# Output stage of a hybrid transformer step: three weight slots instead of four, expert weights requested there one by one

## The chip, the cores and the metric

The kernel runs on one core of one Trainium2 chip. The metric is the device time of one execution in microseconds (us); the figure to compare is the median of several runs. A profile of one execution, with a record of every instruction and DMA packet, stands beside it.

## The reference

One layer of a diffusion backbone in float32, for two streams ("samples") of 128 tokens and 2048 channels:

```
mod = silu(c) @ w_ada + b_ada            # 6 x 2048 values per stream: shift1, scale1, gate1, shift2, scale2, gate2
h   = rmsnorm(x) * (1 + scale1) + shift1
u, q, k, v, g_a, g_b = split(h @ w_in + b_in)
merged = sigmoid(g_a) * (fourier(u) @ w_fourier) + sigmoid(g_b) * (attention(q, k, v) @ w_na_o)
x1  = x + gate1 * (merged @ w_out)                       # the output stage
t   = rmsnorm(x1) * (1 + scale2) + shift2
group = argmax(t @ w_router_group); two best of the 4 experts of that group by t @ w_router_expert
y   = sum over the two experts: weight * ((silu(t @ w_gate[e]) * (t @ w_up[e])) @ w_down[e])
out = rmsnorm(x1 + gate2 * y)
```

There are 16 experts; their three matrices are 4 MB each, 192 MB in all, and every run reads all of them. The rest of the weights is about 220 MB.

## The kernel before, in words

**Dense stages.** Every weight matrix before the experts is read in loads of 1 MB (4 tiles of 128 rows by 512 columns). A load `l` is split by two units, `2*l` and `2*l+1`, of half a load each: ScalarE (ACT) writes the rounded part `w_hi` (`high(u)`, L1370), VectorE (DVE) the remainder `w_lo` (`low(u)`, L1724), and TensorE (PE) multiplies both (`unit(l, half)`, L827 to L829: 12 matmuls of 512 columns). `high(u)` waits until unit `u-4` was used, so ACT and DVE work at most four units ahead. `L_OUT` = 80 is the first load of the output stage `merged @ w_out`, `L_ALL` = 96 the end. Four loads make a chunk of 512 output columns; the stage's chunks are 24 to 27, in banks 0 and 1 or 2 and 3 by turns. When a chunk is complete DVE reads it (`read_chunk`: times gate L1850, plus x L1856), which it counts on `chunk_read`.

**The ring.** Dense loads go to `raw`, four slots of 8 KB a partition (`RAW` = 4). Between them, up to load 77, stands one load of `w_ada` for each dense load: `ada_super(a)` multiplies it with the conditioning vector (L808, 4 matmuls). 64 such loads (a = 32 to 95) share the ring, the last four (a = 92 to 95, `LATE_ADA` = 4) behind the last dense load. Load `n` of the ring has slot `n % 4`, and waits until the slot's previous load was split or multiplied (`slot_released`). SyncE's queue (SP) issues the loads up to 83. From load 84 on ACT issues load `l + 4` in its step `l`, ahead of `high(2*l+4)`.

**Experts.** Expert matrices come in 192 loads of 1 MB in the order in which PE uses them. `MRAW` = 11 slots take them by turns: `mraw` slots 0 to 3 lie over `w_hi` and `w_lo`, 4 to 7 over the four `raw` slots, and `mraw_g`, `mraw_x`, `mraw_y` stand apart. Loads 12 to 15 have single-use places: 12 and 15 in `mraw_a`, 13 and 14 in `mraw_f`, which lies over the upper 16 KB of region F, where `x1T` (the transposed x1) lies too. All are issued by SP in one fixed order (`first_gate_up_load`, L574 on); a wait in it holds up all that stands behind it. From load 11 on each waits until PE has used the load that had its slot (`slot_free`, L546).

**Routing.** x1 is transposed chunk by chunk (`x1_transposes`, L1017; ACT copies it into `x1T`, L1522), and `router(n, s)` (L1027) multiplies chunk `n` of sample `s` with the router's weights, in banks 2 and 3. So `router(0, ...)` first waits until chunk 26 was read out of these banks. After the last load PE does routers 2 and 3, two late `ada_super`, the ranks of the chosen experts (L1109 to L1111), two more `ada_super`, then gathers tokens (L1135) and begins with the experts (gate and up L1196, down L1235, scatter L1277).

Of the kernel before, what the change touches and what calls it, by code (L numbers as in the profile page):

```python
# [13 lines left out]
P = 128  # L14
TOK = 128
# [105 lines left out]
def backbone_step(nc, x_prompt, x_sample, cache_k, cache_v, c, c_ctx, norm1_g, norm2_g, w_ada, b_ada,  # L121
# [24 lines left out]
    with ExitStack() as ctx:  # L146
# [43 lines left out]
        x1T = place("x1T", [P, KD, NS, TOK], F + 16 * KB)  # L190
# [157 lines left out]
        LATE_ADA = 4  # L348
# [10 lines left out]

        def landed_count(n):  # L360

            return 16 * (n // RAW) + 16
# [110 lines left out]
        def slot_released(queue, n):  # L473

            if n >= RAW:
                queue.wait_ge(raw_done[n % RAW], 8 * (n // RAW))

        def ada_super_load(queue, a):

            n = ADA_AT[a]  # L480
            super_chunk, k = GATE1 + (a - A_SUPER) // KD, (a - A_SUPER) % KD
            slot_released(queue, n)
            queue.dma_start(raw[:, n % RAW].rearrange("p (a k) n -> p a (k n)", a=1),
                            ada_v[:, k:k + 1, super_chunk * D:(super_chunk + 1) * D]).then_inc(raw_landed[n % RAW], 16)

        def dense_load(queue, l):

            n = DENSE_AT[l]
            chunk, quad, _ = chunk_of(l)
            if l < L_MERGE:  # L490
                view, col = in_v, PROJ_COLS[chunk]
            elif l < L_OUT:
                i, kind = (chunk - 8) // 4, (chunk - 8) % 4
                view = (in_v, in_v, na_v, fo_v)[kind]
                col = i * COL + (FW + 3 * NA, FW + 3 * NA + D, 0, 0)[kind]
            else:
                view, col = out_v, (chunk - 24) * COL
            slot_released(queue, n)
            queue.dma_start(raw[:, n % RAW], view[:, LOAD_K * quad:LOAD_K * quad + LOAD_K, col:col + COL]
                            ).then_inc(raw_landed[n % RAW], 16)  # L500
# [5 lines left out]
        def _(sp):  # L506
# [67 lines left out]
            with sp.Fori(0, rounds_end) as r:  # L574
# [3 lines left out]

                first_gate_up_load(9)
                first_gate_up_load(10)  # L580
                sp.wait_ge(chunk_read, reads(21))
                first_gate_up_load(8)
                sp.wait_ge(unit_used, 2 * L_ALL - 4)
# [5 lines left out]
                sp.wait_ge(raw_done[0], 8 * (RING_LOADS // RAW))  # L589
# [192 lines left out]
        def _(pe):  # L782
# [13 lines left out]
            def ada_super(a):  # L796

                n = ADA_AT[a]
                super_chunk, k = GATE1 + (a - A_SUPER) // KD, (a - A_SUPER) % KD
                if k == 0:  # L800

                    if super_chunk == GATE1:
                        pe.wait_ge(mod_ready, BLOCKS - 1)
                    else:
                        pe.wait_ge(ada_evac, super_chunk - GATE1)
                pe.wait_ge(raw_landed[n % RAW], landed_count(n))
                for g in range(4):
                    last = nc.tensor.matmul(bank[7][32 * g:32 * g + 32], cpad[:, k], raw[:, n % RAW, g],  # L808
                                            start=k == 0, stop=k == KD - 1)
                last.then_inc(raw_done[n % RAW], 8)  # L810

            def unit(l, half):
# [8 lines left out]
                pe.wait_ge(raw_done[n % RAW], 8 * (n // RAW) + 4 * half + 4)  # L821
# [10 lines left out]
            def last_load(l):  # L832
# [3 lines left out]
                pe.wait_ge(raw_done[n % RAW], 8 * (n // RAW) + 8)  # L836
# [201 lines left out]
            for l in range(L_LOOP, L_ALL - 1):  # L1038
# [37 lines left out]
                if l == L_ALL - 3:  # L1076
                    router(0, 1)
# [26 lines left out]
            for a in (92, 93):  # L1104
                ada_super(a)
# [254 lines left out]
        def _(act):  # L1360
            step = Tally(act, act_step)
            def high(u):

                n = DENSE_AT[u // 2]
                if u % 2 == 0:
                    act.wait_ge(raw_landed[n % RAW], landed_count(n))
                if u >= AHEAD:
                    act.wait_ge(unit_used, u - AHEAD + 1)
                r = raw[:, n % RAW, (u % 2) * UNIT_K:(u % 2) * UNIT_K + UNIT_K]
# [74 lines left out]
            def super_done(super_chunk):  # L1444

                n = ADA_AT[A_SUPER + KD * (super_chunk - GATE1) + KD - 1]
                act.wait_ge(raw_done[n % RAW], 8 * (n // RAW) + 8)
# [72 lines left out]
            def x1_transposed(n, s):  # L1520
                act.wait_ge(x1T_done, 2 * n + s + 1)
                nc.scalar.activation(x1T[:, 4 * n:4 * n + 4, s], bank[x1T_bank(n, s)][:].rearrange("p (k t) -> p k t", k=4), ACT.Copy  # L1522
# [192 lines left out]
        def _(dve):  # L1715
# [3 lines left out]
            def low(u):  # L1719
# [3 lines left out]
                r = raw[:, n % RAW, (u % 2) * UNIT_K:(u % 2) * UNIT_K + UNIT_K]  # L1723
                v.tensor_tensor(w_lo[:, u % AHEAD], r, w_hi[:, u % AHEAD].bitcast(F32), ALU.subtract  # L1724
                                ).then_inc(raw_done[n % RAW], 4)
# [393 lines left out]
            dve.wait_ge(raw_done[n % RAW], 8 * (n // RAW) + 8)  # L2119
# [185 lines left out]
```

## Time and profile before

| | us |
|---|---|
| three runs, median | 1196.16 |
| three runs, lowest and highest | 1195.09, 1196.16 |
| the profiled execution, its own time | 1196.65 |
| span of the profile, first to last instruction | 1194.8 |
| PE busy (5577 matmul records) | 1116.9 (93%) |
| DVE busy, ACT busy | 535.9, 366.3 |
| 64 `in_w_in` loads, issue to landing (median) | 8.3 |
| 46 `in_w_exp_gate` loads, issue to landing (median) | 20.8 |

Positions such as "at 680 us" count from the span's start. Busy time of PE is overlapped time of pipelined matmuls: 0.39 us is the duration of a 512-column matmul, but in a dense row of them one starts every 0.23 us (the 12 of a half load take 2.73 us). A float32 matmul stands in the trace as two records, so the 8 matmuls of two `ada_super` appear as x16. Idle time of an engine that nobody waits for costs nothing. "GB/s" is what all 16 DMA engines of the core moved together.

### The profile page before, as it was taken

The page shows a single profiled execution, that of the slowest core. Times are in us where ns is not written, and L with a number is a line of the kernel's source. Part 1 is how long each engine was busy: PE and PEld are TensorE (multiplying, and loading weights), DVE is VectorE, ACT ScalarE, POOL GpSimd, SP SyncE. Part 2 cuts the span into 40 slices and gives each one's busy share as a digit, 9 for nine tenths or more (in the row PEclk, how much of TensorE's full clock was granted, in tenths as well). Part 3 has the DMA queues.
Part 4 walks back from the last instruction along what each step waited for, and adds up shares of the span by engine and source line. Part 5 has one row for each costly group of instructions (what it writes and reads, how often), then busy time and mean ns, then how long its engine had stood idle before and what let it go on. Part 6 is the DMA issues. An engine that isn't in the chain of part 4 may idle for free.

```text
span 1194.8 us, 14481 instructions
## 1 busy us (share of the span) xinstructions
PE 1116.9 (93%) x5577; PEld 682.5 (57%) x5577; DVE 535.9 (45%) x781; ACT 366.3 (31%) x526; POOL 54.8 (5%) x100
## 2 busy tenths in 40 slices
PE   5899999999999999999999999999999888988795
PEld 2566766777777677667788875434344234423231
DVE  0464575555455444454466755242416041504056
ACT  3342342444433333333345533320112001201023
POOL 0210200110000220000010100000000000000000
PEclk9999999999999999999999999999999999999997
DMA  9999978887877898888898799999999999999994
GB/s 357 385 386 381 364 286 320 312 302 281 286 289 283 306 351 323 326 299 319 329 362 260 219 381 423 390 415 423 423 423 423 423 422 424 422 423 423 423 406 174
DMA packets 114964, 423.22 MB, mean 354 GB/s; under 512 B 9088, under 2 KB 9264, under 8 KB 82640
## 3 DMA queue, kind: packets, MB, share of 16 engines
q1 hardware_dynamic: 101968, 389.57, 83.4%
q0 software_dynamic: 5424, 15.35, 4.8%
q10 hardware_dynamic: 7504, 17.37, 4.0%
q8 instruction: 45, 0.74, 0.2%
q14 instruction: 23, 0.19, 0.0%
HBM read 418.27 MB, written 3.98 MB: 353 GB/s over the span
## 4 chain that ended last, share of the span: by engine, by line
PE 69%; DMA 27%; SPq 1%; DVE 1%; issue 1%; ACT 1%; DVEq 0%
PE bank L827 14%; PE bank L828 13%; PE bank L829 13%; PE bank L1196 10%; DMA mraw<-in_w_exp_up 10%; DMA mraw<-in_w_exp_down 5%; PE bank L808 5%; DMA raw<-in_w_in 4%; DMA mraw<-in_w_exp_gate 4%; PE bank L1235 3%; DMA raw<-in_w_ada 2%; PE bank L1135 2%; DMA mraw_y<-in_w_exp_gate 2%; PE bank L792 1%; PE bank L1277 1%; PE bank L1258 1%
## 5 line engine op out<-in xcount | busy, mean ns | idle before, releaser
L1724 DVE TENSOR_TENSOR w_lo<-raw,w_hi 128x1024 fp32r<-128x1024 f32 x192 | 231.8, 1223 | 246.7 <-ACT w_hi L1370 245.6
L1370 ACT ACTIVATE w_hi<-raw 128x1024 fp32r<-128x1024 f32 x192 | 200.3, 1057 | 313.3 <-DMA raw<-in_w_in 160.4
L827 PE MATMUL bank<-w_hi,h_hi 128*128 128x512 f32 x512 | 206.2, 403 | 6.6 <-DVE w_lo L1724 4.3
L828 PE MATMUL bank<-w_lo,h_hi 128*128 128x512 f32 x512 | 200.1, 391 | 0.0
L829 PE MATMUL bank<-w_hi,h_lo 128*128 128x512 f32 x512 | 199.8, 390 | 0.0
L1196 PE MATMUL bank<-mraw,xg 128*64 128x512 f32 x720 | 184.9, 597 | 12.5 <-DMA mraw<-in_w_exp_gate 4.8
L827 PEld LDWEIGHTS bank<-w_hi,h_hi 128*128 128x128 f32 x512 | 96.2, 188 | 47.1 <-issue 24.8
L1196 PEld LDWEIGHTS bank<-mraw,xg 128*64 128x64 f32 x720 | 57.7, 136 | 108.4 <-issue 105.6
L829 PEld LDWEIGHTS bank<-w_hi,h_lo 128*128 128x128 f32 x512 | 96.1, 188 | 21.0
L828 PEld LDWEIGHTS bank<-w_lo,h_hi 128*128 128x128 f32 x512 | 96.3, 188 | 18.1
L2190 DVE SCALAR_TENSOR_TENSOR d_lo<-bank,slot_w,d_hi 128x512 fp32r<-128x512 f32 x32 | 23.9, 747 | 161.6 <-ACT d_hi L1669 161.0
L1235 PE MATMUL bank<-mraw,hidT 128*64 128x512 f32 x336 | 84.3, 607 | 12.2 <-DMA mraw<-in_w_exp_down 12.2
L1669 ACT ACTIVATE d_hi<-bank,slot_w 128x512 fp32r<-128x512 f32 x32 | 22.0, 688 | 226.8 <-PE bank L1235 142.3
L2202 DVE TENSOR_TENSOR bank<-bank,ga2b 128x512 f32<-128x512 f32 x64 | 41.5, 694 | 77.1 <-PE bank L1277 77.0
L808 PE MATMUL bank<-raw,cpad 128*32 128x512 f32 x512 | 63.3, 610 | 2.8 <-DMA raw<-in_w_ada 2.8
L1235 PEld LDWEIGHTS bank<-mraw,hidT 128*64 128x64 f32 x336 | 26.9, 139 | 57.2 <-issue 52.7
L792 PE MATMUL bank<-araw,cpad 128*32 128x512 f32 x256 | 34.2, 643 | 14.8 <-DMA araw<-in_w_ada 14.8
L827 PE MATMUL bank<-w_hi,m_hi 128*128 128x512 f32 x120 | 47.7, 398 | 0.0
L829 PE MATMUL bank<-w_hi,m_lo 128*128 128x512 f32 x120 | 46.9, 390 | 0.0
L828 PE MATMUL bank<-w_lo,m_hi 128*128 128x512 f32 x120 | 46.7, 390 | 0.0
L2129 DVE TENSOR_TENSOR xg<-bank,rbi 128x512 f32<-128x512 f32 x32 | 21.9, 684 | 52.8 <-PE bank L1135 52.8
L1196 PE MATMUL bank<-mraw_g,xg 128*64 128x512 f32 x96 | 43.7, 598 | 1.6 <-DMA mraw_x<-in_w_exp_up 1.2
(293 smaller groups left out, 1332.2 us busy)
## 6 DMA issues: line engine op xcount, KB each, us to landing
raw<-in_w_in SPq DMA_DIRECT2D x64, 1024.0 KB, 8.3
raw<-in_w_ada SPq DMA_DIRECT2D x60, 1024.0 KB, 8.2
mraw<-in_w_exp_gate SPq DMA_DIRECT2D x46, 1024.0 KB, 20.8
mraw<-in_w_exp_up SPq DMA_DIRECT2D x44, 1024.0 KB, 20.9
mraw<-in_w_exp_down SPq DMA_DIRECT2D x42, 1024.0 KB, 20.6
araw<-in_w_ada SPq DMA_DIRECT2D x64, 512.0 KB, 10.9
raw<-in_w_out ACTq DMA_DIRECT2D x12, 1024.0 KB, 9.3
raw<-in_w_na_o SPq DMA_DIRECT2D x8, 1024.0 KB, 7.2
```

The source lines that it names most:

```text
L792: last = nc.tensor.matmul(bank[7 - b % 2][32 * g:32 * g + 32], cpad[:, 2 * j + g % 2], araw[:, n % ARAW, g], start=j == 0, stop=j == 7)
L808: last = nc.tensor.matmul(bank[7][32 * g:32 * g + 32], cpad[:, k], raw[:, n % RAW, g], start=k == 0, stop=k == KD - 1)
L827: nc.tensor.matmul(o, hi[:, k, s], wh, start=k == first, stop=False)
L828: nc.tensor.matmul(o, hi[:, k, s], wl, start=False, stop=False)
L829: last = nc.tensor.matmul(o, lo[:, k, s], wh, start=False, stop=k == final)
L1135: last = nc.tensor.matmul(out[:, kk * EPG * CAP:(kk + 1) * EPG * CAP], (t_hi, t_lo)[part][:, s, k * P:(k + 1) * P], pick[:, s, g * EPG:(g ...
L1196: last = nc.tensor.matmul(out[x * CAP:(x + 1) * CAP], xg[:, q * LOAD_K + kk, e * CAP:(e + 1) * CAP], slab(2 * unit + x)[:, kk * COL:(kk + ...
L1235: last = nc.tensor.matmul(bank[first_bank + n][x * CAP:(x + 1) * CAP], hidT[:, i % 2, k, x * CAP:(x + 1) * CAP], slab(2 * unit + x)[:, n * ...
L1370: nc.scalar.activation(w_hi[:, u % AHEAD], r, ACT.Copy).then_inc(hi_ready, 1)
L1724: v.tensor_tensor(w_lo[:, u % AHEAD], r, w_hi[:, u % AHEAD].bitcast(F32), ALU.subtract).then_inc(raw_done[n % RAW], 4)
L2190: v.scalar_tensor_tensor(out=d_lo[:, c % 2], in0=bank[first_bank + n][:], scalar=slot_w[:, i:i + 1], in1=d_hi[:, c % 2].bitcast(F32), op0= ...
L2202: v.tensor_tensor(bank[out + s][:], bank[out + s][:], ga2b[:, s, cols], ALU.mult).then_inc(y_scaled, 1)
```

## The change

1. `x1T` shrinks from 16 chunk-tiles to 8: chunk `n` goes to half `n % 2`. The upper 8 KB of `mraw_f` (the place of expert load 14) are no longer under `x1T`.
2. From the first output load on (ring place `DENSE_AT[80]`) the ring turns over three slots. Slot 3 ends with `ada_super(92)`, and expert load 7, which lies over it, can come early.
3. `LATE_ADA` is 3: load 92 of `w_ada` moves from behind the dense loads to the pair of load 78, and its `ada_super` from behind the routers into the step of load 78.
4. SP asks for expert loads 9, 10, 8 at given points of the output stage (`unit_used` 172, 174, 178, not at once), and then for 14 and 7 (182 and 184), which before came after the routers.
5. `router(0, 0)` and `router(0, 1)`, before in the two halves of load 93, now both stand after the first half of load 92, since chunk 2 will overwrite chunk 0's half of `x1T`.

```diff
-        x1T = place("x1T", [P, KD, NS, TOK], F + 16 * KB)
+        x1T = place("x1T", [P, 2 * 4, NS, TOK], F + 16 * KB)
...
-        LATE_ADA = 4
+        LATE_ADA = 3
...
+        RING_CUT = DENSE_AT[L_OUT]
+        ring_slots = [n % RAW if n < RING_CUT else (n - RING_CUT + RING_CUT % RAW) % (RAW - 1) for n in range(RING_LOADS)]
+
+        def ring_slot(n):
+            return ring_slots[n]
+
+        def ring_turn(n):
+            return ring_slots[:n].count(ring_slots[n])
+
+        def slot_end(slot):
+            return 8 * ring_slots.count(slot)
...
-            if n >= RAW:
-                queue.wait_ge(raw_done[n % RAW], 8 * (n // RAW))
+            if ring_turn(n):
+                queue.wait_ge(raw_done[ring_slot(n)], 8 * ring_turn(n))
...
+                sp.wait_ge(unit_used, 2 * L_OUT + 12)
                 first_gate_up_load(9)
+                sp.wait_ge(unit_used, 2 * L_OUT + 14)
                 first_gate_up_load(10)
                 sp.wait_ge(chunk_read, reads(21))
+                sp.wait_ge(unit_used, 2 * L_OUT + 18)
                 first_gate_up_load(8)
+                sp.wait_ge(chunk_read, reads(22))
+                sp.wait_ge(unit_used, 2 * L_OUT + 22)
+                first_gate_up_load(14)
+                sp.wait_ge(raw_done[RAW - 1], slot_end(RAW - 1))
+                sp.wait_ge(unit_used, 2 * L_OUT + 24)
+                first_gate_up_load(2 * RAW - 1)
                 sp.wait_ge(unit_used, 2 * L_ALL - 4)
                 first_gate_up_load(15)
                 for n in (0, 2, 1, 3):
                     sp.wait_ge(unit_used, 2 * L_ALL - 2 + n % 2 * 2)
                     first_gate_up_load(n)
                 first_gate_up_load(12)
-                sp.wait_ge(raw_done[0], 8 * (RING_LOADS // RAW))
+                sp.wait_ge(raw_done[0], slot_end(0))
                 first_gate_up_load(RAW)
                 sp.wait_ge(route_done, NS)
                 first_gate_up_load(13)
-                first_gate_up_load(14)
-                for n in range(1, RAW):
-                    sp.wait_ge(raw_done[n], 8 * (RING_LOADS // RAW))
+                for n in range(1, RAW - 1):
+                    sp.wait_ge(raw_done[n], slot_end(n))
                     first_gate_up_load(RAW + n)
...
-                    last = nc.tensor.matmul(bank[2 + s][:, 0:NG + NE], x1T[:, k, s], gw[:, s, k],
+                    last = nc.tensor.matmul(bank[2 + s][:, 0:NG + NE], x1T[:, k % 8, s], gw[:, s, k],
...
-                if l == L_ALL - 3:
+                if l == L_ALL - 4:
                     router(0, 0)
+                    router(0, 1)
...
-                if l == L_ALL - 3:
-                    router(0, 1)
...
-            for a in (92, 93):
-                ada_super(a)
+            ada_super(93)
```

In the program as built, PE's rows around the second half of load 92 are these before (the L1017 row are the transposes behind load 92's second half; the L1027 row is `router(0, 0)`, after the first half of load 93; 12 matmul rows are one half load):

```order
2399 L829 MATMUL bank<-w_hi,m_lo 128x512
2400 L1017 MATMUL bank<-cst_all,x_67 128x128 x4
2401 L827 MATMUL bank<-w_hi,m_hi 128x512
...
2412 L829 MATMUL bank<-w_hi,m_lo 128x512
2413 L1027 MATMUL bank<-gw,x1T 128x20 x4
2414 L827 MATMUL bank<-w_hi,m_hi 128x512
```

and these in the changed kernel:

```order
2388 L852 MATMUL bank<-w_hi,m_lo 128x512
2389 L1050 MATMUL bank<-gw,x1T 128x20 x8
2390 L850 MATMUL bank<-w_hi,m_hi 128x512
2391 L851 MATMUL bank<-w_lo,m_hi 128x512
...
2401 L852 MATMUL bank<-w_hi,m_lo 128x512
2402 L1040 MATMUL bank<-cst_all,x_67 128x128 x4
```

Both routers of chunk 0 now stand 12 matmuls ahead of the transposes, the first of them 24 matmuls and the transposes earlier than before.

SP's queue from the last dense loads to the first load that waits for an expert's slot, before:

```order
149 L499 DMA raw<-in_w_out 128x4x512 x4
151 L535 DMA mraw_x<-in_w_exp_gate 128x2048
152 L535 DMA mraw_y<-in_w_exp_up 128x2048
153 L535 DMA mraw_g<-in_w_exp_gate 128x2048
154 L535 DMA mraw_a<-in_w_exp_up 128x2048
...
159 L535 DMA mraw_a<-in_w_exp_gate 128x2048
160 L535 DMA mraw<-in_w_exp_gate 128x2048
161 L535 DMA mraw_f<-in_w_exp_gate 128x2048
162 L535 DMA mraw_f<-in_w_exp_up 128x2048
163 L535 DMA mraw<-in_w_exp_gate 128x2048
164 L535 DMA mraw<-in_w_exp_up 128x2048 x2
```

and in the changed kernel:

```order
153 L550 DMA mraw_x<-in_w_exp_gate 128x2048
154 L550 DMA mraw_y<-in_w_exp_up 128x2048
155 L550 DMA mraw_g<-in_w_exp_gate 128x2048
156 L550 DMA mraw_f<-in_w_exp_up 128x2048
157 L550 DMA mraw<-in_w_exp_up 128x2048
158 L550 DMA mraw_a<-in_w_exp_up 128x2048
...
163 L550 DMA mraw_a<-in_w_exp_gate 128x2048
164 L550 DMA mraw<-in_w_exp_gate 128x2048
165 L550 DMA mraw_f<-in_w_exp_gate 128x2048
166 L550 DMA mraw<-in_w_exp_gate 128x2048
167 L550 DMA mraw<-in_w_exp_up 128x2048
```

Loads 14 (`mraw_f<-in_w_exp_up`) and 7 (`mraw<-in_w_exp_up`) went from the end of this group to the place behind load 8.

## Rows read from the trace of the kernel before

**Rows 1.** Page, DMA and TensorE's granted clock in 40 slices of 29.9 us.
```profile
PEclk9999999999999999999999999999999999999997
DMA  9999978887877898888898799999999999999994
GB/s 357 385 386 381 364 286 320 312 302 281 286 289 283 306 351 323 326 299 319 329 362 260 219 381 423 390 415 423 423 423 423 423 422 424 422 423 423 423 406 174
```

**Rows 2.** Busy time by stretch: us, PE, PEld, DVE, ACT, POOL, PEclk, DMA share, GB/s.
```profile
605.00:700.00 95.00, 95.00 (x452) 79.23 (x452) 58.47 (x61) 47.20 (x58) 9.63 (x18) 1.00 0.85 286
720.00:755.00 35.00, 35.00 (x184) 15.02 (x182) 12.79 (x29) 9.59 (x18) 0.00 (x0) 1.00 1.01 422
755.00:785.00 30.00, 30.00 (x159) 13.24 (x157) 6.04 (x9) 10.85 (x21) 0.00 (x0) 1.00 0.96 382
785.00:830.00 45.00, 45.00 (x222) 18.98 (x220) 18.50 (x29) 8.20 (x16) 0.00 (x0) 1.00 1.01 423
830.00:1150.00 320.00, 284.23 (x1313) 114.12 (x1311) 93.86 (x147) 41.12 (x78) 0.00 (x0) 0.99 1.01 423
```

**Rows 3.** Waits of SP's queue between 714 and 830 us: us in total, times, longest.
```profile
SPq L546 <- PE bank L1196: 76.8, 18, 10.2
SPq L546 <- PE bank L1235: 14.6, 5, 4.7
```

**Rows 4.** Chain that ended last: start us, us, what.
```profile
574.92 1.85 PE bank L808 x16
...
728.86 7.02 PE bank L1196 x32
...
739.69 13.88 PE bank L1196 x64
...
829.77 15.40 DMA mraw<-in_w_exp_up
...
882.05 3.63 PE bank L1235 x16
...
1014.40 5.35 PE bank L1235 x16
```

**Rows 5.** Timeline of DVE: start us, us, engine, line, operation, tiles.
```profile
678.67 1.23 DVE L1724 TENSOR_TENSOR w_lo<-raw,w_hi 128x1024 fp32r<-128x1024 f32 x1 [1.44 <-ACT w_hi L1370]
681.13 0.68 DVE L1850 TENSOR_TENSOR gab<-gab,bank 128x512 f32<-128x512 f32 x1
681.96 0.69 DVE L1856 TENSOR_TENSOR x<-x,gab 128x512 f32<-128x512 f32 x1 [0.15 <-DVE gab L1850]
710.76 0.19 DVE L2090 TENSOR_TENSOR chosen<-sel 128x32 f32<-128x32 f32 x1
```

**Rows 6.** Timeline of PE, loads 92 and 93, then the end of routing.
```profile
680.02 0.39 PE L827 MATMUL bank<-w_hi,m_hi 128*128 128x512 f32 x1
682.75 0.60 PE L1017 MATMUL bank<-cst_all,x 128*128 128x128 f32 x4
685.94 0.96 PE L1027 MATMUL bank<-gw,x1T 128*128 128x20 f32 x8
686.75 0.49 PE L827 MATMUL bank<-w_hi,m_hi 128*128 128x512 f32 x1
...
704.16 1.86 PE L1027 MATMUL bank<-gw,x1T 128*128 128x20 f32 x16
706.34 2.24 PE L1027 MATMUL bank<-gw,x1T 128*128 128x20 f32 x16
708.51 3.23 PE L808 MATMUL bank<-raw,cpad 128*32 128x512 f32 x16
711.66 0.41 PE L1109 MATMUL bank<-chosen,cst_route 128*128 128x32 f32 x2
712.45 1.92 PE L808 MATMUL bank<-raw,cpad 128*32 128x512 f32 x16
```

**Rows 7.** Busy time by stretch around the two falls of the granted clock.
```profile
708.00:711.00 3.00, 3.00 (x15) 1.06 (x19) 2.46 (x10) 1.94 (x7) 0.00 (x0) 0.50 1.01 418
1012.40:1014.30 1.90, 0.00 (x0) 0.00 (x0) 0.00 (x0) 0.00 (x0) 0.00 (x0) 1.00 1.02 423
1015.00:1018.00 3.00, 3.00 (x10) 0.94 (x7) 0.75 (x1) 1.00 (x2) 0.00 (x0) 0.50 1.00 418
```

**Rows 8.** One issue each, to landing: expert load at 778.5 us, `w_ada` load at 677.5.
```profile
DMA to landing us min/median/max: 6.2/6.2/6.2
...
DMA to landing us min/median/max: 4.7/4.7/4.7
```

**Rows 9.** DVE and ACT around load 89; issue to landing of loads 89 and 84; page, issues.
```profile
638.32 2.35 DVE L1724 TENSOR_TENSOR w_lo<-raw,w_hi 128x1024 fp32r<-128x1024 f32 x2
...
639.30 0.37 ACTq L499 DMA_DIRECT2D raw<-in_w_out  x1
652.12 1.06 ACT L1370 ACTIVATE w_hi<-raw 128x1024 fp32r<-128x1024 f32 x1 [1.24 <-PE bank L829]
...
DMA to landing us min/median/max: 11.4/11.4/11.4
DMA to landing us min/median/max: 12.1/12.1/12.1
...
raw<-in_w_out ACTq DMA_DIRECT2D x12, 1024.0 KB, 9.3
```

**Rows 10.** Timeline of SP's queue: expert loads 9 and 4.
```profile
601.23 0.36 SPq L535 DMA_DIRECT2D mraw_x<-in_w_exp_gate  x1
...
710.50 0.33 SPq L535 DMA_DIRECT2D mraw<-in_w_exp_gate  x1
```

More of the change, by code:

```diff
@@ L482, in ada_super_load @@
             slot_released(queue, n)
-            queue.dma_start(raw[:, n % RAW].rearrange("p (a k) n -> p a (k n)", a=1),
-                            ada_v[:, k:k + 1, super_chunk * D:(super_chunk + 1) * D]).then_inc(raw_landed[n % RAW], 16)
+            queue.dma_start(raw[:, ring_slot(n)].rearrange("p (a k) n -> p a (k n)", a=1),
+                            ada_v[:, k:k + 1, super_chunk * D:(super_chunk + 1) * D]).then_inc(raw_landed[ring_slot(n)], 16)
         def dense_load(queue, l):
@@ L498, in dense_load @@
             slot_released(queue, n)
-            queue.dma_start(raw[:, n % RAW], view[:, LOAD_K * quad:LOAD_K * quad + LOAD_K, col:col + COL]
-                            ).then_inc(raw_landed[n % RAW], 16)
+            queue.dma_start(raw[:, ring_slot(n)], view[:, LOAD_K * quad:LOAD_K * quad + LOAD_K, col:col + COL]
+                            ).then_inc(raw_landed[ring_slot(n)], 16)
         block = ctx.enter_context(nc.Block())
@@ L805, in ada_super @@
                         pe.wait_ge(ada_evac, super_chunk - GATE1)
-                pe.wait_ge(raw_landed[n % RAW], landed_count(n))
+                pe.wait_ge(raw_landed[ring_slot(n)], landed_count(n))
                 for g in range(4):
-                    last = nc.tensor.matmul(bank[7][32 * g:32 * g + 32], cpad[:, k], raw[:, n % RAW, g],
+                    last = nc.tensor.matmul(bank[7][32 * g:32 * g + 32], cpad[:, k], raw[:, ring_slot(n), g],
                                             start=k == 0, stop=k == KD - 1)
-                last.then_inc(raw_done[n % RAW], 8)
+                last.then_inc(raw_done[ring_slot(n)], 8)
             def unit(l, half):
@@ L819, in unit @@
                           (o_hi, o_lo) if (chunk - 8) % 4 == 2 else (f_hi, f_lo))
-                pe.wait_ge(raw_done[n % RAW], 8 * (n // RAW) + 4 * half + 4)
+                pe.wait_ge(raw_done[ring_slot(n)], 8 * ring_turn(n) + 4 * half + 4)
                 for t in range(UNIT_K):
@@ L835, in last_load @@
                 n = DENSE_AT[l]
-                pe.wait_ge(raw_done[n % RAW], 8 * (n // RAW) + 8)
+                pe.wait_ge(raw_done[ring_slot(n)], 8 * ring_turn(n) + 8)
                 for s in range(NS):
@@ L1365, in high @@
                 if u % 2 == 0:
-                    act.wait_ge(raw_landed[n % RAW], landed_count(n))
+                    act.wait_ge(raw_landed[ring_slot(n)], landed_count(n))
                 if u >= AHEAD:
                     act.wait_ge(unit_used, u - AHEAD + 1)
-                r = raw[:, n % RAW, (u % 2) * UNIT_K:(u % 2) * UNIT_K + UNIT_K]
+                r = raw[:, ring_slot(n), (u % 2) * UNIT_K:(u % 2) * UNIT_K + UNIT_K]
                 nc.scalar.activation(w_hi[:, u % AHEAD], r, ACT.Copy).then_inc(hi_ready, 1)
@@ L1521, in x1_transposed @@
                 act.wait_ge(x1T_done, 2 * n + s + 1)
-                nc.scalar.activation(x1T[:, 4 * n:4 * n + 4, s], bank[x1T_bank(n, s)][:].rearrange("p (k t) -> p k t", k=4), ACT.Copy
+                nc.scalar.activation(x1T[:, n % 2 * 4:n % 2 * 4 + 4, s], bank[x1T_bank(n, s)][:].rearrange("p (k t) -> p k t", k=4), ACT.Copy
                                      ).then_inc(x1T_ready, 1)
@@ L1722, in low @@
                 dve.wait_ge(hi_ready, u + 1)
-                r = raw[:, n % RAW, (u % 2) * UNIT_K:(u % 2) * UNIT_K + UNIT_K]
+                r = raw[:, ring_slot(n), (u % 2) * UNIT_K:(u % 2) * UNIT_K + UNIT_K]
                 v.tensor_tensor(w_lo[:, u % AHEAD], r, w_hi[:, u % AHEAD].bitcast(F32), ALU.subtract
-                                ).then_inc(raw_done[n % RAW], 4)
+                                ).then_inc(raw_done[ring_slot(n)], 4)
             def chained(ins):
@@ L2118, in _ @@
             n = ADA_AT[95]
-            dve.wait_ge(raw_done[n % RAW], 8 * (n // RAW) + 8)
+            dve.wait_ge(raw_done[ring_slot(n)], 8 * ring_turn(n) + 8)
             dve.wait_ge(bias2_row_in, 64)
```

4 lines of the change are left out of this document (2 added, 2 removed).

## The prediction

> **What bounds the kernel now.** I first read the page's slices [rows 1]: the DMA moves 423 GB/s in nearly every slice of the last 40%, and in two slices ahead of it, in the output stage, 260 and 219. That invites moving transfers forward, which is what the change does: loads 14 and 7 and one load of w_ada, 3 MB. The table by stretch [rows 2] splits this further. From 605 to 700 us PE is busy without a gap (95.00 of 95.00) while the DMA moves 286 GB/s: PE bounds the output stage, and whatever is put on it is paid in full. From 830 to 1150 the DMA runs at 423 and PE is busy for 284 of 320 us: the DMA bounds. The stretch between decides what the change is worth. From 720 to 830 PE is busy all the time, so PE bounds, and from 755 to 785 the DMA falls to 382 GB/s. SP's waits tell why [rows 3]: between 714 and 830 SP waits 76.8 + 14.6 us for PE to free a slot. The DMA is as far ahead there as eleven slots allow. In the chain [rows 4] the first long wait for an expert load is the one issued at 829.77.
>
> So the end is set like this: PE's progress up to about 785 us says when slots come free; from the last moment at which the DMA queue ran low (near 778) it runs at full rate to the end. A later PE in 600 to 780 moves the end; an earlier transfer moves it only by what the queue still held at 778.
>
> **Part by part.**
>
> *Loads 14 and 7 early, and one late w_ada load fewer.* At 423 GB/s [rows 2] 1 MB (1.049 million bytes) takes 2.48 us, so 7.4 us of transfers leave the stretch after 700 us. The lead is lost where the slots are full. What can be kept: the load issued at 778.5 us landed after 6.2 us, one issued to an idle DMA after 4.7 us [rows 8]. With an empty queue it would land 1.5 us sooner, and with it all that follow. Bounds: 0 (the restart takes 6.2 us anyhow) and -1.5. I take **-1.0**, nearer to the row of the idle DMA, as the queue will be empty there.
>
> *ada_super(92) moved into load 78.* A pair costs PE 1.85 us [rows 4], one 0.93. PE has no gap there, so **+0.93**. What is saved: after the routers the pair 92, 93 took from 708.51 to 711.66, at a granted clock of 0.50 [rows 6, 7]. The choice of experts was ready at 710.95 (710.76 + 0.19) [rows 5], and the rank matmuls began at 711.66. With one ada_super they can begin at about 711.05: **-0.6**. The rest of that pair was covered by DVE's choice.
>
> *router(0, 0) and router(0, 1) after the first half of load 92.* Their 0.81 us each (685.94 to 686.75) [rows 6] stay in PE's row, so moving costs nothing. But the first waits for chunk 26 to be read from banks 2 and 3. PE began the second half of load 92 at 680.02 [rows 6]. DVE first finished a split (678.67 to 679.90), since its queue holds low(187) ahead of the read, and ended the second multiplication that empties the banks at 681.81 (681.13 + 0.68); the next step behind that semaphore began at 681.96 [rows 5]. PE will stand from 680.02 to about 681.95: **+1.93**. Before, this wait was met 5.9 us later (685.94) and cost nothing. Its place relative to unit 183, which releases the split in DVE's queue, is fixed, so the wait doesn't shrink as the stage shifts. Behind it in PE's queue stands everything up to the experts. DVE and ACT are paced by PE, so nothing is made good.
>
> *The clock.* Behind that gap PE runs 16 router matmuls, 2 x 0.81 us, before dense work returns. The granted clock was at 0.50 (1.2 of 2.4 GHz) twice: from 708, behind the router matmuls from 704.16 on, and from 1015, behind a stop that covers 1012.40 to 1014.30 and ended at 1014.40, about 2.05 us [rows 4, 6, 7]. Here gap and routers come in a row, 3.6 us of little work. I take it that the clock falls once. Price: the group of 16 down records took 5.35 us at 1014.40 where its like at 882.05 took 3.63 [rows 4]: **+1.7**. Bounds 0 and +1.8.
>
> *Three ring slots.* ACT issued load l+4 in step l, when its slot (load l) had long been split. Now the slot is load l+1's, and ACT waits for low(2l+3): issue up to 2.4 us later (one split on ACT, 1.06, and one on DVE, 1.23 [rows 5, 9]). Queued behind it is high(2l+4), due 2.7 us after the previous one, so it loses at most 0.1 us. Load 89, the slowest, was issued at 639.30, took 11.4 us, and its first split began at 652.12 [rows 9]: 1.4 us to spare. PE reaches that unit three half loads later (3 x 2.73 us [rows 6]), and needs the split 2.5 us ahead: 5.6 us more, 7.0 in all. Late issue (1.4 us for this load, since DVE's split ends at 640.7) and one expert load in its way (2.48) leave 3.1. I take **0**; the cover is ACT's and DVE's lead of four units. If it is gone, PE waits.
>
> There is a rule against this part. By the Trainium skill (DMA: Bandwidth & Descriptors, Issuing engines are not separate DMA queues) DMAs issued from different engines run on the same 16 engines and interleave; by it the spread expert loads slow the w_out loads just when their lead shrinks. The trace agrees: load 84, issued at 609.12 with three expert loads and x on their way, took 12.1 us, against a median of 9.3 for these loads [rows 9]. By the rule without the slack the five loads would cost up to 5 x 2.48 us.
>
> *SP's new waits.* Load 9 was issued at 601.23 [rows 10]; 9, 10 and 8 now come 40 to 60 us later, but are first used at 739.69 [rows 4]: 0. Load 4 waited for the slot of ada_super(92) and was issued at 710.50 [rows 10]. Now slot 0 ends with ada_super(94), done near 713.4 (half of the pair from 712.45 [rows 6]); behind it in SP's queue stand 13, 5 and 6. Load 4, 13, 5 land at about 718.1, 720.6 and 723.1 on an idle DMA, and 4 and 5 are first used at 728.86 [rows 4]. 5.7 us to spare: 0.
>
> **Sum.** 0.93 - 0.6 + 1.93 + 1.7 = 3.96 us later on PE, less 1.0 = **+2.96 us**. The profiled execution took 1196.65, so 1199.6; it stands 0.5 above the runs' median of 1196.16, so the forecast for the median is **1199.1**. About 0.2% (2.4 us) is what a measurement of this kernel can tell from no change.
>
> **Rivals.**
>
> A. *The wait comes, the clock holds.* +1.26: 1197.4. For it: the fall at 1015 followed a complete stop of 2.05 us, the coming one is 1.93 and then there is some work. Against: routers alone preceded the fall at 708. The Trainium skill (TensorE: Matmul & The Clock Gate, What's actually happening) calls the throttled state the default, released by activity; by it gap plus thin matmuls speak for the fall, as the 0.50 from 708 does [rows 7]. Chance 0.22.
>
> B. *The router's wait costs nothing,* as DVE reads chunk 26 earlier than I think. 0.93 - 0.6 - 1.0: 1195.5. Against: DVE's queue is in fixed order, and nothing of it moves. Chance 0.12.
>
> C. *The transfers count in full* (the other side: faster). If the DMA bounded from 715 us on, all 3 MB would be taken from the end: +3.96 - 7.44 = -3.5, 1192.7, or 1191.0 with the clock held. For it: 423 GB/s and a PE that waits after 830 [rows 2]. It decides where the DMA never runs low between 715 and 785. Against: 382 GB/s and SP's 91 us of waiting for slots [rows 2, 3]. Chance 0.07.
>
> D. *Starved output stage.* More than 3.1 us of extra latency on some w_out load makes PE wait in the stage that has no gap. One expert load's time more, 2.5 us: 1201.6 and above. For it: 11.4 us of latency with no expert load in the stage. Chance 0.09.
>
> Forecast: 0.50.
>
> **How the numbers follow.** Range: the forecast's own bounds are 1198.1 (clock 1.2, as part of the slow stretch may fall on the routers, lead -1.5) and 1200.2 (1.8 and 0); A and B are to be inside, the near edge of D too: 1195.3 to 1201.2. Faster by over 0.2% (below 1193.8): C and little of B, 0.08. Slower (above 1198.6): four fifths of the forecast, all of D, a little of A: 0.52. Within: 0.40.
>
> **What would show it.** In the changed profile PE should stand still for about 1.9 us just before 16 router records, with DVE's second gate multiplication of chunk 26 ending there; the granted clock should read 0.5 for some 3 us behind it; the rank matmuls should begin 0.1 us behind the choice of experts; between 755 and 785 us GB/s should be below 382, and SP's waits on L546's successor longer by about what was moved forward; from 830 on DMA at 423 and PE waiting as before. Router and rank should stand 3 to 4.5 us later than now, the first down quarter about 3 us. Wrong would be: no stop ahead of the routers (B), 423 GB/s through 755 to 785 (C), or waits of PE for w_lo between 605 and 700 (D).

## The result and the profile after

| | before | changed |
|---|---|---|
| five runs each, taken together, median us | 1196.16 | 1201.84 |
| lowest and highest | 1195.09, 1196.32 | 1200.99, 1204.24 |
| ratio of the times, with 95% interval | | 1.0052 (1.0037 to 1.0066) |
| the profiled execution, its own time and span | 1196.65, 1194.8 | 1204.24, 1202.4 |

The change costs 5.7 us. The direction is the forecast one, the size is almost double (+2.96), and 1201.84 lies 0.6 above the top of the range (1201.2). The profiled execution of the changed kernel is the slowest of its five, so its profile shows more than the median: 7.6 us. Of all runs named below three took 2.9 to 3.5 ms, in a slow state; ratios and averages of clocks leave them out.

First the page's slices, 30.1 us each (before: [rows 1]):

```profile
PEclk9999999999999999999999989999999999999997
GB/s 359 385 386 379 362 286 322 313 301 279 273 279 287 331 356 318 297 329 323 329 265 304 337 290 411 353 410 422 424 423 424 423 422 423 423 424 422 423 405 156
```

The two thin slices of the output stage are filled (260 and 219 have become 304 and 337), and the bytes are missing on both sides: 265 for 362 just ahead, since loads 9, 10 and 8 come later, and 290 and 353 where 381 and 390 stood. A clock of 8 is new in the 24th slice (691 to 721 us). Next the timeline of PE around the early routers (start us, us, engine, line, operation, tiles, count, idle time before it with its releaser):

```profile
680.96 0.39 PE L852 MATMUL bank<-w_hi,m_lo 128*128 128x512 f32 x1
683.09 2.08 PE L1050 MATMUL bank<-gw,x1T 128*128 128x20 f32 x16 [1.74 <-DVEq L1875]
685.00 0.78 PE L850 MATMUL bank<-w_hi,m_hi 128*128 128x512 f32 x1
685.58 0.63 PE L851 MATMUL bank<-w_lo,m_hi 128*128 128x512 f32 x1
...
688.41 0.39 PE L852 MATMUL bank<-w_hi,m_lo 128*128 128x512 f32 x1
```

That is the forecast stop: a matmul that would have begun 0.23 us after 680.96 begins after 2.13, so 1.90 us are lost. The 16 router records (8 matmuls) follow, and then dense matmuls of 0.63 instead of 0.39 us. DVE's second multiplication of chunk 26 ends where the prediction put it, 0.12 us ahead of the routers (682.29 + 0.68):

```profile
679.83 1.23 DVE L1745 TENSOR_TENSOR w_lo<-raw,w_hi 128x1024 fp32r<-128x1024 f32 x1 [1.32 <-ACT w_hi L1391]
682.29 0.68 DVE L1871 TENSOR_TENSOR gab<-gab,bank 128x512 f32<-128x512 f32 x1
```

The end of routing, same columns (before: [rows 6]):

```profile
711.03 2.58 PE L1050 MATMUL bank<-gw,x1T 128*128 128x20 f32 x16
713.54 1.94 PE L831 MATMUL bank<-raw,cpad 128*32 128x512 f32 x8
716.04 0.64 PE L1130 MATMUL bank<-chosen,cst_route 128*128 128x32 f32 x2 [0.56 <-DVE chosen L2111]
...
717.46 3.64 PE L831 MATMUL bank<-raw,cpad 128*32 128x512 f32 x16
721.03 1.22 PE L1167 MATMUL bank<-pick,rr 128*128 128x256 f32 x4
...
726.22 1.08 PE L1217 MATMUL bank<-mraw,xg 128*64 128x512 f32 x4
```

Here is what the prediction didn't have. The one multiplication left behind the routers took 1.94 us, and the pair 94, 95 took 3.64 where 1.92 stood before. The table by stretch (us, then PE, PEld, DVE, ACT, POOL busy, granted clock, DMA share, GB/s) says why:

```profile
684.80:688.20 3.40, 3.40 (x11) 2.72 (x11) 1.36 (x2) 0.00 (x0) 1.45 (x3) 0.50 0.99 390
708.00:712.00 4.00, 4.00 (x36) 3.87 (x35) 2.64 (x7) 2.25 (x8) 0.00 (x0) 1.00 0.79 264
712.20:722.20 10.00, 9.44 (x42) 4.62 (x43) 7.05 (x23) 2.43 (x7) 0.00 (x0) 0.50 0.74 285
722.50:726.00 3.50, 3.50 (x31) 3.50 (x30) 2.32 (x4) 3.46 (x7) 0.00 (x0) 1.00 0.99 419
755.00:785.00 30.00, 30.00 (x159) 13.15 (x157) 6.04 (x9) 11.57 (x22) 0.00 (x0) 1.00 0.88 351
...
700.00:720.00 20.00, 19.44 (x108) 14.22 (x110) 10.75 (x32) 5.50 (x15) 0.00 (x0) 0.80 0.79 306
...
763.00:765.00 2.00, 2.00 (x12) 0.64 (x10) 0.17 (x1) 1.79 (x2) 0.00 (x0) 1.00 0.01 4
...
830.00:1150.00 320.00, 283.18 (x1316) 113.59 (x1312) 89.25 (x139) 39.74 (x76) 0.00 (x0) 1.00 1.01 423
```

The clock is at 0.50 from 684.8 to 688.2, as forecast, and then from 712.1 to 722.3: 10.2 us, where before it was 3.4 us behind the same routers (a stretch at 0.50 is called slow from here on). The head start has become idle time of the DMA, much of it early: from 700 to 720 its share is 0.79, where the kernel before has 1.00,

```profile
700.00:720.00 20.00, 19.29 (x135) 14.16 (x135) 14.54 (x37) 9.28 (x22) 0.00 (x0) 0.91 1.00 403
```

and expert load 4, which waits for the slot of `ada_super(94)`, was issued at 719.46 (before 710.50). From 755 to 785 the share is 0.88 (before 0.96), and from 763 to 765 the DMA stood still. SP's waits between 714 and 830 us for PE to free a slot are about as long as before [rows 3], and the loads issued at 764.47 (to the idle DMA) and at 785.05 took, from issue to landing:

```profile
SPq L561 <- PE bank L1217: 74.9, 17, 10.0
SPq L561 <- PE bank L1256: 11.9, 4, 4.7
...
DMA to landing us min/median/max: 4.8/4.8/4.8
DMA to landing us min/median/max: 7.5/7.5/7.5
```

The 7.6 us of this profile come out so. Up to the second half of load 92: 681.19 - 680.02 = +1.17, of it 0.93 for the multiplication in load 78. The wait: +1.90. From there to the last 16 router matmuls, with the first slow stretch in it: 27.94 against 26.32, +1.62. From those to the first expert matmul: 15.19 against 13.32, +1.87. From that to the end: 476.18 against 475.14, +1.0.

### The profile page after: what moved, and what is told of

Read it like the earlier page. It is cut to its first block, busy times and chain, and to the rows that moved or that the text cites. A ratio compares the mean times of both kernels' runs of the same rounds, so it can differ in the third digit from the quotient of the medians.

```text
span 1202.4 us, 14484 instructions
## 1 busy us (share of the span) xinstructions
PE 1120.4 (93%) x5577; PEld 684.8 (57%) x5577; DVE 536.2 (45%) x781; ACT 366.2 (30%) x526; POOL 54.6 (5%) x100
## 4 chain that ended last, share of the span: by engine, by line
PE 69%; DMA 26%; SPq 2%; DVE 1%; issue 1%; ACT 1%; DVEq 0%
PE bank L850 14%; PE bank L851 13%; PE bank L852 13%; PE bank L1217 10%; DMA mraw<-in_w_exp_up 6%; PE bank L831 5%; DMA mraw<-in_w_exp_down 5%; DMA mraw<-in_w_exp_gate 3%; DMA raw<-in_w_in 3%; PE bank L1256 3%; PE bank L1156 2%; DMA raw<-in_w_ada 2%; DMA mraw_y<-in_w_exp_gate 2%; DMA mraw_g<-in_w_exp_up 2%; DMA mraw_x<-in_w_exp_down 2%; SPq L584 1%
```

## The experiments

Beside each group of experiments the kernel before ran on the same chip: median 1196.68 beside the first four, 1196.83 beside the next four, 1195.87 beside the last three (23 to 29 runs each). The ratio given isn't the quotient of the two medians; the two differ by up to 0.1%. "Router-to-expert time" below is from the start of the last 16 router matmuls to the first expert matmul: 13.32 before, 15.19 changed.

**Early routers behind the second half of load 92** (the changed kernel otherwise).

```diff
@@ after unit(l, 0) @@
-                if l == L_ALL - 4:
-                    router(0, 0)
-                    router(0, 1)
@@ after unit(l, 1), ahead of the transposes @@
+                if l == L_ALL - 4:
+                    router(0, 0)
+                    router(0, 1)
```

> The changed kernel with router(0, 0) and router(0, 1) put behind the second half of load 92, ahead of the transposes; nothing else. If PE's wait for the reading of chunk 26 and the fall of the clock behind it are the main cost, both go: 1.9 + 1.7 us less than the changed kernel's 1201.8, so 1198.2. If the three slots, or the expert loads in the output stage, are what costs, it stays at 1201.8.

Measured 1199.23, ratio 1.0017 (1.0008 to 1.0027). PE has no stop in the output stage and no slow stretch there; the last router matmuls began at 706.78 (before 706.34). So the place of the early routers is most of the loss. But the router-to-expert time stayed 15.19, with 10.2 slow us from 707.9:

```profile
709.24 1.94 PE L831 MATMUL bank<-raw,cpad 128*32 128x512 f32 x8
...
713.16 3.64 PE L831 MATMUL bank<-raw,cpad 128*32 128x512 f32 x16
```

What happens behind the routers doesn't need the stop.

**The same placement put into the kernel before.**

```diff
-                if l == L_ALL - 3:
+                if l == L_ALL - 4:
                     router(0, 0)
+                    router(0, 1)
...
-                if l == L_ALL - 3:
-                    router(0, 1)
```

> The kernel before, with router(0, 0) and router(0, 1) moved behind the first half of load 92 as in the change; nothing else. If wait and clock are a cost of their own: 1196.2 + 1.9 + 1.7 = 1199.8; if the wait comes and the clock holds, 1198.1; if the three slots are needed for the damage, 1196.2.

Measured 1201.8, ratio 1.0034 (1.0022 to 1.0045). By the medians this one edit costs 5.1 us, nearly what the change costs; by the ratios, 1.0034 to 1.0052, two thirds of it. The timeline of PE:

```profile
679.99 0.39 PE L829 MATMUL bank<-w_hi,m_lo 128*128 128x512 f32 x1
682.12 2.58 PE L1027 MATMUL bank<-gw,x1T 128*128 128x20 f32 x16 [1.74 <-DVEq L1853]
684.52 0.77 PE L827 MATMUL bank<-w_hi,m_hi 128*128 128x512 f32 x1
```

The wait is the same: 1.74 idle, 1.90 lost. The slow stretch behind it, from 683.3, lasted 6.8 us here, and from the first router to the last 16 router records it took 29.5 us; with 3.4 slow us it takes 27.9. So the length isn't fixed, and each 3.4 slow us are about 1.6 us of time.

**Transfers 14 and 7 asked for late again** (the changed kernel otherwise).

```diff
-                sp.wait_ge(chunk_read, reads(22))
-                sp.wait_ge(unit_used, 2 * L_OUT + 22)
-                first_gate_up_load(14)
-                sp.wait_ge(raw_done[RAW - 1], slot_end(RAW - 1))
-                sp.wait_ge(unit_used, 2 * L_OUT + 24)
-                first_gate_up_load(2 * RAW - 1)
...
+                first_gate_up_load(14)
+                for n in range(1, RAW):
```

> The changed kernel with expert loads 14 and 7 asked for behind load 13 and load 6, as before the change. If a full set of slots eats any head start, it is within 1 us of the changed kernel's 1201.8 (and if an empty DMA queue restarts badly, 1 us faster). If early transfers carry through to the end, it is 2 x 2.48 = 5 us slower, 1206.8. If they disturb the output stage, it is faster by what they disturb, over 1 us, and PE's waits for w_lo between 605 and 700 us go away with them.

Measured 1203.05, ratio 1.0046 (1.0029 to 1.0063), against 1.0052 with them early: the 5 us of a full gain are ruled out, a gain of 1 or 2 us isn't (six runs). The DMA's share from 700 to 720 and from 755 to 785 us is 0.87 and 1.00 here, against 0.79 and 0.88 with them early. From the first expert matmul to the end it took 475.8 (476.2 with them early).

**Early routers moved and the multiplication of load 92 back behind the routers** (load 14 early, load 7 late; of the edit only the lines of the multiplication are shown).

```diff
-            return [A_SUPER + i for i in pair if i < L_LAST_ADA - LATE_ADA - L_LOOP]
+            return [A_SUPER + i for i in pair if i < L_LAST_ADA - 4 - L_LOOP]
...
-            ada_super(93)
+            for a in (92, 93):
+                ada_super(a)
```

> The changed kernel with the routers of chunk 0 behind the second half of load 92, and the multiplication of w_ada load 92 back behind the routers (its load stays where the change has it, so expert load 7 comes late as before; load 14 stays early). If wait, clock and the added multiplication are all that costs, this is back at 1196.2 within 1 us. If the three slots cost by themselves, it stays above 1198.

Measured 1196.79, ratio 0.9998 (0.9988 to 1.0008): the whole loss is gone. In this profile PE had no stop at all and yet 10.2 slow us behind the routers, with a router-to-expert time of 15.78:

```profile
708.54 3.64 PE L828 MATMUL bank<-raw,cpad 128*32 128x512 f32 x16
712.11 0.64 PE L1128 MATMUL bank<-chosen,cst_route 128*128 128x32 f32 x2
```

So a long slow stretch needs neither the stop nor three late multiplications. But the profiled execution, 1199.71, is the second slowest of twelve, and their median doesn't pay for such a stretch.

**Only three late multiplications, in the kernel before.**

```diff
-        LATE_ADA = 4
+        LATE_ADA = 3
...
-            for a in (92, 93):
-                ada_super(a)
+            ada_super(93)
```

> The kernel before with LATE_ADA = 3 alone (load 92 of w_ada and its multiplication at load 78, one multiplication instead of two behind the routers); routers, four slots and the order of the expert loads as before. By the prediction's terms: 0.93 - 0.3 (as measured in the changed kernel) = +0.6, 1196.9. If the stop of 0.6 us that one multiplication leaves behind the routers also makes the clock's slow stretch there longer (10.2 us instead of 3.4, worth 1.9 us from the last router to the first expert matmul), the median is 1198 to 1199 and more than half of the runs stand above 1197.7. If the move is free, 1196.2.

Measured 1199.46, ratio 1.0011 (1.0001 to 1.002); the medians lie 2.6 us apart, the ratio says 1.3. The timeline of PE:

```profile
707.65 1.92 PE L1027 MATMUL bank<-gw,x1T 128*128 128x20 f32 x16
709.50 1.06 PE L808 MATMUL bank<-raw,cpad 128*32 128x512 f32 x8
712.03 0.41 PE L1108 MATMUL bank<-chosen,cst_route 128*128 128x32 f32 x2 [1.46 <-DVE chosen L2089]
...
716.56 0.63 PE L1134 MATMUL bank<-pick,t_hi 128*128 128x256 f32 x2
...
720.84 1.94 PE L1195 MATMUL bank<-mraw,xg 128*64 128x512 f32 x8
```

The rank came 4.38 us behind the last router matmuls instead of 5.32, but the slow stretch (from 713.9) now fell on the gathering (0.63 for 0.40). The router-to-expert time, 13.19, is as before. The multiplication fewer saved 0.1 us there and cost 0.93 in the stage. The time is that of the longer stretch, which was expected at 1198 to 1199 (10 of 11 runs stand above 1197.7), but this profile doesn't show it.

**Also load 14 late**, leaving three slots, the halved `x1T` and the spaced requests: the kernel of the fourth experiment, with the early request for 14 taken out as well.

> As e3_both (routers later, multiplication 92 back), and expert load 14 late too, so that no transfer is early and only the three slots, the halved x1T and the spaced requests are left. If early transfers are worth nothing and three slots cost nothing: 1196.2 to 1196.8, as e3_both. If load 14's early transfer was worth its 2.5 us: 1199.3. If three slots had been paid back by it: the same.

Measured 1196.5, ratio 0.9997 (0.9986 to 1.0008). Three slots cost nothing that can be measured. No slow stretch fell behind the routers in this profile, and it shows the floor:

```profile
707.48 1.93 PE L826 MATMUL bank<-raw,cpad 128*32 128x512 f32 x16
710.01 0.41 PE L1126 MATMUL bank<-chosen,cst_route 128*128 128x32 f32 x2 [0.61 <-DVE chosen L2107]
...
713.34 0.71 PE L1163 MATMUL bank<-pick,rr 128*128 128x256 f32 x4 [0.62 <-DVE pick L2128]
...
717.93 4.94 PE L1213 MATMUL bank<-mraw,xg 128*64 128x512 f32 x22
```

The last router matmuls stand at 705.63, so the rank again came 4.38 us later, with two multiplications between as with one. In the profiles with a full clock there DVE's choice sets this, and PE waits for it.

**Expert loads 9, 10 and 8 asked for at once** (the changed kernel without the three spacing waits).

```diff
-                sp.wait_ge(unit_used, 2 * L_OUT + 12)
                 first_gate_up_load(9)
-                sp.wait_ge(unit_used, 2 * L_OUT + 14)
                 first_gate_up_load(10)
                 sp.wait_ge(chunk_read, reads(21))
-                sp.wait_ge(unit_used, 2 * L_OUT + 18)
                 first_gate_up_load(8)
```

> The changed kernel with expert loads 9, 10 and 8 asked for as soon as SP comes to them, as before the change, not at units 172, 174 and 178. Under the theory that PE alone sets the pace there: 1201.8 as the changed kernel, within 1 us, and PE without waits for w_lo between 605 and 680. If the spacing disturbs the w_out loads: faster by more than 1 us; if it protects them: slower by more than 1 us.

Measured 1205.93, ratio 1.0063 (1.005 to 1.0077). PE's waits from 600 to 700 us (total, times, longest), and issue to landing of the `w_out` load issued at 613.14:

```profile
PE bank L1047 <- DVEq L1872: 1.7, 1, 1.7
PE bank L1037 <- DVE x L1874: 1.4, 1, 1.4
PE bank L847 <- DVE w_lo L1742: 1.1, 1, 1.1
...
DMA to landing us min/median/max: 19.0/19.0/19.0
```

Only the first of the three waits stands in the changed kernel. The two new ones are the starved output stage of rival D, and the spacing prevents it. The kernel before asks for these loads at once too, with four slots, and its PE has no wait from 605 to 706 us. The cost of leaving out the spacing isn't shown in the time: the intervals 1.005 to 1.0077 and 1.0037 to 1.0066 overlap. By the Trainium skill (DMA: Bandwidth & Descriptors, Issuing engines are not separate DMA queues) loads of SP and ACT share the 16 engines and interleave; the 19.0 us against 12.1 for the slowest in the changed kernel agree.

**Matmuls that keep PE dense behind the routers.** To the first experiment's kernel, matmuls of 128x512 on data at rest were added, whose result nobody reads: three behind the multiplication of load 93 and two behind 95.

```diff
+            def dense_filler(count):
+                for _ in range(count):
+                    nc.tensor.matmul(bank[6][:], m_hi[:, 4, 0], m_hi[:, 4:6].rearrange("p k s t -> p (k s t)"),
+                                     start=True, stop=True)
...
+            dense_filler(3)
```

> As e1_routers_later, with 3 matmuls of 128 by 128 by 512 whose result nobody reads put behind multiplication 93 and 2 behind 95, where PE stands idle 0.6 and 0.7 us at full clock. If the slow stretch behind the routers is longer because PE does little there, dense work shortens it and the median falls from 1199.2 to about 1197.5, in spite of the added work. If the length of the stretch is set by something else, the fillers only add their time: up to 1 us slower than e1_routers_later.

Measured 1197.67, ratio 1.001 (0.9999 to 1.0022). No slow stretch fell behind the routers, and the router-to-expert time was 12.30:

```profile
707.99 1.92 PE L1050 MATMUL bank<-gw,x1T 128*128 128x20 f32 x16
709.84 1.07 PE L831 MATMUL bank<-raw,cpad 128*32 128x512 f32 x8
710.83 0.96 PE L1131 MATMUL bank<-m_hi 128*128 128x512 f32 x3
712.37 0.41 PE L1138 MATMUL bank<-chosen,cst_route 128*128 128x32 f32 x2 [0.58 <-DVE chosen L2120]
...
713.16 1.92 PE L831 MATMUL bank<-raw,cpad 128*32 128x512 f32 x16
```

The multiplication alone takes 1.07 us here and 1.94 in the changed kernel. But the clock was full at 708 already, ahead of them, where it had fallen in the first experiment, so this one profile doesn't show them to be the cause; and the intervals of the two experiments overlap, so a gain isn't shown either.

**Eight such matmuls in the 1.9 us wait** of the changed kernel, ahead of `router(0, 0)`.

> The changed kernel with 8 matmuls of 128 by 128 by 512, whose result nobody reads, in PE's row ahead of the two early routers, where it stands still 1.9 us: 8 x 0.23 = 1.8 us, so the wait stays and the idleness goes. If the clock falls there because PE does nothing, it no longer falls and this is 1.7 to 3.4 us faster than the changed kernel: 1198.5 to 1200. If the fall comes from the thin router matmuls alone, it stays at 1201.8.

Measured 1201.69, ratio 1.0044 (1.0031 to 1.0057). The timeline of PE and the stretch behind:

```profile
681.96 1.98 PE L1065 MATMUL bank<-m_hi 128*128 128x512 f32 x8
683.86 1.96 PE L1050 MATMUL bank<-gw,x1T 128*128 128x20 f32 x16
685.67 0.48 PE L850 MATMUL bank<-w_hi,m_hi 128*128 128x512 f32 x1
...
684.80:688.20 3.40, 3.40 (x21) 2.96 (x21) 2.13 (x3) 0.00 (x0) 2.13 (x4) 1.00 1.00 417
```

With the wait filled, the clock stays at 1.00 behind it, and from the first router to the last 16 router records it took 26.35 us (27.94 with the slow stretch). So this profile puts the first fall down to the idle time, not to the routers alone. But the 1.7 to 3.4 us expected didn't come: the ratios are 1 us apart, and the intervals overlap. The same profile has 10.2 slow us behind the routers.

**Four such matmuls in the kernel before** (two behind the pair 92, 93 and two behind 94, 95), **and in the kernel of the sixth experiment.**

> The kernel before with two such matmuls behind multiplications 92 and 93 and two behind 94 and 95. The profile of before has a slow stretch of 3.4 us behind the routers, and from the last router to the first expert matmul it took 13.3 us against 12.3 in the two profiles without a slow stretch there. If dense work in PE's row shortens the stretch, up to 1 us faster: 1195.2 to 1196.2. If it only adds time, up to 1 us slower.

> e6_both_transfers_late (three slots, spaced requests, routers of chunk 0 behind the second half of load 92, multiplication 92 back, no early transfer) with the fillers of e10_before_filler. Candidate for a version better than both: 1195.5 if the fillers hold the clock, 1196.5 to 1197.3 if they only cost.

Measured 1196.5, ratio 1.0007 (0.9997 to 1.0017), and 1196.89, ratio 1.0008 (0.9997 to 1.0018): nothing. Both profiles had a slow stretch of 3.4 us from about 708 all the same; it begins with the router matmuls, ahead of what was added. No version beats the kernel before.

All thirteen profiles in one table:

| slow us behind the routers | router-to-expert us | kernels |
|---|---|---|
| 0 | 12.3 | 6th; 8th (matmuls added to the 1st) |
| 3.4 | 13.2 to 13.8 | before; 2nd (early routers in it); 5th (three late in it); the last two |
| 6.8 | 13.8, 13.9 | 3rd (transfers late); 7th (asked at once) |
| 10.2 | 15.2 to 15.8 | changed; 1st; 4th; 9th (wait filled) |

From the first expert matmul to the end it took 475.6 us on average over the five kernels with both transfers early (475.0 to 476.2) and 475.6 over the seven with both late (474.3 to 476.7). From 755 to 785 us the DMA's share is 0.86 to 0.88 in those five, 0.92 with one of the two early, and 0.95 to 1.00 in the seven.

A profile is one execution, but every run has its mean granted clock on record. It goes with the time: of 80 runs of the kernel before, the 28 at 0.994 took 1196.1 us on average, the 9 at 0.990 or less 1199.1. The averages of 5 to 12 runs each (in brackets the 23 to 29 of the kernel before on the same chip), uncertain by 0.0003 to 0.0010; "ahead" means ahead of the second half of load 92, where the stop is:

| kernel | early routers | late multiplications | mean granted clock |
|---|---|---|---|
| changed; 3rd; 7th; 9th | ahead | 3 | 0.9892; 0.9892 (0.9927); 0.9885 (0.9923); 0.9888 (0.9934) |
| 2nd | ahead | 4 | 0.9902 (0.9927) |
| 1st; 5th | no stop | 3 | 0.9911 (0.9927); 0.9907 (0.9923) |
| 8th, with added matmuls | no stop | 3 | 0.9924 (0.9923) |
| 4th; 6th | no stop | 4 | 0.9928 (0.9927); 0.9927 (0.9923) |
| last two, with added matmuls | no stop | 4 | 0.9924; 0.9930 (0.9934) |

Early routers ahead of the wait go with a lower clock, and so do three late multiplications instead of four (only the eighth experiment, with matmuls added, doesn't show it). By an estimate from the two levels, 1.00 and 0.50, 0.0016 less over 1197 us is 3.8 us more at 0.50. With the wait filled the average is no higher (0.9888 against 0.9892).

## Why the prediction was off

**What bounds, and the wait of the early routers: right.** The stop came at its place, behind the releaser named, with 1.90 us for a forecast 1.93. The experiment that removed it and the one that put it into the kernel before show it to be, together with the clock behind it, the largest part: +3.4 in a thousand by itself, and -3.5 (1.0052 to 1.0017) when undone.

**The clock in the output stage: right in kind, the size at its lower end.** It fell once, and cost 1.6 us (27.94, and 27.89 in the seventh experiment, against 26.35 with the wait filled) for a term of 1.7. But in two of the four profiles with the stop it stayed down for 6.8 us, which is 3.2. The upper bound of 1.8 was taken from one fall [rows 4], as if each lasted 3.4 us.

**The multiplication in load 78: right.** 1.17 us of shift for 0.93. The 0.24 left over are no more than the shift of 0.2 and 0.3 that the profiles of the second and tenth experiment show near the same place without this multiplication.

**"With one ada_super they can begin at about 711.05: -0.6": wrong.** The term took the chosen experts' time of [rows 5] as fixed and PE as what was late. In the profiles with a full clock there the rank comes 4.38 us behind the start of the last router matmuls, when DVE's choice is there, whether one or two multiplications stand between (the timelines of the fifth and sixth experiment), so at full clock there is nothing to save. In the changed kernel the rank came 0.31 us sooner (5.01 for 5.32), and more than that was lost behind it: where the clock is down, PE's matmuls here take twice as long. In the changed kernel even the routers took 2.58 us (2.24 before), the pair 94, 95 3.64, and the piece cost +1.87. The prediction priced the fall in the output stage and took the fall at 708 for constant. It grew from 3.4 to 10.2 us. In the profiles 10.2 us is found in three of seven kernels with three late multiplications and in one of six with four, and one profile of each can't tell. The times and clocks of all runs say more: the two kernels with four put back and no stop stand at 1196.8 and 1196.5, with the average clock of the kernel before, the two with three and no stop at 1199.2 and 1199.5, with a clock lower by 0.0016. By the medians that is some 1.7 us over the kernel before beyond the 0.93 that the multiplication costs by itself, by the ratios 0.4 to 1.1; 3.8 slow us more, at 1.6 us for each 3.4, are 1.8 (an estimate). So three late multiplications instead of four bring more slow time, where nothing is added to fill it. Where in the program it falls, and why, stays open: the clock of a run is on record only as a mean.

**"I take -1.0, nearer to the row of the idle DMA": wrong.** The rest of that paragraph held: the lead was lost, and the DMA idled more (0.88 for 0.96, and ahead of that 0.79 for 1.00). The queue did run empty, but the load behind the restart took 7.5 us, longer than the 6.2 of [rows 8], and the one that met an idle DMA, 4.8, stood 20 us earlier, where it decided nothing. Five kernels against seven give 0.0 from the first expert matmul to the end.

**What was to be seen.** The 382 GB/s fell to 351, and the rank began 0.06 us behind the choice (715.79 + 0.19 to 716.04), as forecast; router and rank stood 4.7 and 4.4 us later for "3 to 4.5", and the first down quarter 6.6 (781.30 for 774.75) for "about 3". SP's waits for slots were to grow and did not (74.9 + 11.9 us for 76.8 + 14.6): the same slots come free at the same steps of PE, and the time that was moved forward shows as idle DMA instead.

**Three slots, SP's waits: right**, 0 each. Load 4 came at 719.46 and not near 713.4, and still PE waited for no expert load up to 829 us. Load 89 was not the slowest: the one issued at 621.17 took 12.4 us. Rival D's mechanism is real and was shown, but the spacing that stands in the diff keeps it away.

So the sum of +2.96 should have read 1.17 + 1.90 + 1.6 to 3.2 + 0 to 1.9 + 0, which is 4.7 to 8.2, with the bounds of the clock taken from single profiles; the median of 5.7 and the profile's 7.6 (with its +1.0 behind the first expert matmul) lie in it. The runs of the changed kernel have on average 0.0035 less clock than the kernel before: 8.4 slow us more, some 3.9 us by the same estimate. The prediction had 1.7 for this. Its two misses are the clock, priced as one fall of fixed length, and the savings of 0.6 and 1.0, which weren't there.

## What to carry to other kernels

A transfer moved forward is worth only what is left of the lead where buffers last run full; work out that place first, and put no bonus on it. When thin work is moved next to a wait, look for who reads the bank last, and try the place one half load later: here that alone was worth two thirds of the loss (by the ratios, 1.0052 to 1.0017). And when a kernel already has a stretch of low granted clock, don't carry it over as a constant: price it at zero and at several times its length. One profile doesn't tell which of these the median pays; the mean clock of all runs does.

## What the runs showed of the chip

- A stop of 1.74 us and 16 router records of 20 columns behind it were followed by a granted clock of 0.50 (1.2 of 2.4 GHz) in all four profiles that had them. With the stop filled it stayed at 1.00 (one profile), and so it did in the five profiles in which the same 16 records stood in a row without a stop. By the Trainium skill (TensorE: Matmul & The Clock Gate, What's actually happening) the low state is the default and activity releases it. The traces agree with the direction.
- The stretches at 0.50 in 600 to 1150 us lasted 3.4, 6.8 or 10.2 us, and the same instructions of PE ahead of them gave different lengths (3.4 us behind the stop in the changed kernel, 6.8 in the third experiment). PE was busy nearly all the time in the changed kernel's long one (9.44 of 10.00 us), with the matmuls of routing and of `w_ada`, so a busy PE row doesn't say that the clock is coming back.
- A 1 MB load to an idle DMA landed after 4.8 us, one behind the restart of the queue after 7.5, and a `w_out` load after 19.0 where three expert loads were asked for at once. The kernel before has 4.7 and 6.2 for the first two [rows 8].
